# Gates to rows and back by small transfers and block transposes, in a hybrid attention block

## The chip, the core and the metric

One Trainium2 chip; the kernel runs on one of its cores. The metric is device time in microseconds of one execution. A core has five engines that are named here as the profile names them: PE (TensorE, matrix products; PEld is its weight loads), DVE (VectorE), ACT (ScalarE), POOL (GpSimd) and SP (SyncE). Each runs its own queue of instructions in order, and they wait for each other by semaphores. POOL and SP also issue transfers (DMA) on queues of their own.

## What is computed

The reference is one block of a network: a root mean square norm of x (256 tokens of 4096), a projection into three kinds of token mixing (an mLSTM, a sparse attention, a gated delta rule), and a projection back that is added to x.

```python
h = rms_norm(x, norm_g[l])
proj = jnp.einsum('bsd,dn->bsn', h, w_in[l])
(aq, ak, av, ai, af, ao, az, bcq, bk, bv, bki, bwi, bz,
 cqkv, cb, ca, cz) = jnp.split(proj, split_points, axis=-1)
h_a = mlstm_chunked(..., soft_cap(ai + m_ib[l]), soft_cap(af + m_fb[l]))
...
beta = jax.nn.sigmoid(cb)
g = -jnp.exp(d_a_log[l]) * jax.nn.softplus(ca + d_dt_bias[l])
o_c = gated_delta_chunked(q_c, k_c, v_c, g, beta)
...
x = x + jnp.einsum('bsm,md->bsd', y, w_out[l])
```

The gates ai, af, cb and ca are 8 columns each, one for each head. They need running sums and maxima over the 256 tokens, and end as factors of one token and one head.

## The kernel before

**Chunks and gaps.** The work is a list of 46 blocks of matrix product, each over 512 columns (496 for the block with the gates), cut into 536 chunks of two 128-row slices of the weights. A chunk is 12 matmuls on PE: two slices, two halves of the tokens, and three products of high and low parts (L1039, L1041, L1042). SP loads raw weights (w_raw, four buffers). ACT rounds them to w_hi (`split_hi`, L1313), DVE makes the rest w_lo (`split_lo`, L1650), both three chunks ahead of PE and with four buffers, so ACT can make w_hi of chunk c+3 only when PE has done with chunk c-1. Products go to two accumulators; after a block's last chunk ACT reads its accumulator with the norm's factor (`evac`).

**What sets the order.** `plan` writes everything else by hand into gaps: `woven[c]` lists the pieces that stand after chunk c on every engine. In slot c ACT first does w_hi of c+3, then its parts of the pieces of `woven[c]`; DVE likewise with w_lo; PE does chunk c and then its parts. `weave(at, pieces, every)` puts pieces in gaps from `at` on. `end(kind)` is the last chunk of a block. The block with the gates is block 6 and ends with chunk 111; block 7, the first of two with a Silu, ends with chunk 127.

**The pieces around the change.** `evac` of block 6 writes the gates to `small` (128 tokens on partitions, 2 halves, 112 columns). `csq` and `cn` take squares of q and k and sum them on PE; ACT's part of cn i is a Ln of PE's sum (L1428). `ce` takes Exp on ACT (L1432) and multiplies on DVE (L1807, L1809). The gates go through seven steps:
- gt: PE turns `small` by eight transposes into rows (L1010), one head on each of 8 partitions and 256 tokens along it; ACT reads them from PE's banks with Tanh, Exp, Identity and Ln (L1375 to L1387) into `rows`.
- g1 (DVE, with a reciprocal, L1710 to L1713), g2 (ACT, Exp and Ln, L1391, L1392), g3 (DVE, running sums and maxima, L1719 to L1736), g4 (ACT, two Exp, L1396, L1399).
- gb: PE turns `rows` back by nine transposes; DVE copies them to `gcol` (L1740), and with ACT makes `gder`.

POOL writes rows 1 to 3 to `rows_dram` (L812) when g3 is done and spreads them to all partitions for `ca` (L818, L819). ca, cg, vd, kn and all that follow, down to a place in block 15, are laid out from where gb stands. Ahead of that POOL moves the values of the heads to memory and back for a block transpose (v_dram, L800, L805), in two halves `hg`. ACT loads a table of functions before Tanh or Exp, before Ln and before Silu when another is in place.

```python
def gt(_, use):                       # PE
    wait_stored(pe, "gates", 512)
    for i in range(4):
        u = use + i // 2
        ...
        for m in range(M):
            ins = turn(bank(u)[0:8, (i % 2) * SEQ + m * P:(i % 2) * SEQ + m * P + P],
                       small[:, m, 8 * i:8 * i + 8])
```

## Time and profile before

| what | us |
|---|---|
| median of three timed runs | 1539.94 (1539.55 to 1540.01) |
| the profiled execution | 1541.16 |
| its span | 1539.4 |
| PE busy | 1534.1 |
| DVE busy | 994.4 |
| ACT busy | 753.0 |
| POOL busy | 353.2 |

The profile is of one execution. A timeline gives the instructions of an engine in order of their start; matmuls are pipelined, so their lengths overlap and the cost of one is read from the starts. In brackets stands how long the engine was idle before an instruction and what released it. The granted clock of PE was full in every slice.

### The profile page before, as it was taken

The numbers are of one execution on the slowest core, as the hardware profiler recorded it, in microseconds if no ns is written. First come the engines' busy times: TensorE is split into PE (matmuls) and PEld (weight loads), VectorE is DVE, ScalarE is ACT, GpSimd is POOL, SyncE is SP. The second block draws the span as 40 slices with busy tenths as digits, with TensorE's granted clock in tenths as the row PEclk, the third lists the DMA queues.
The fourth block names the chain that finished last, engine by engine and source line by source line (L and its number), as shares of the span: only waits on it lengthen the run. The fifth ranks groups of instructions, "written<-read, shape, count | busy, mean of one in ns | idle before, by whom it ended". The sixth has DMA issues, their size and how long they took to land.

```text
span 1539.4 us, 18848 instructions
## 1 busy us (share of the span) xinstructions
PE 1534.1 (100%) x7000; PEld 1271.0 (83%) x7000; DVE 994.4 (65%) x1536; ACT 753.0 (49%) x1006; POOL 353.2 (23%) x601
## 2 busy tenths in 40 slices
PE   9999999999999999999999999999999999999999
PEld 7888888888888888888878888888888888888887
DVE  6647555657769855576579667675456676664554
ACT  6745444587543444554545545535346444443332
POOL 8041112230230040127410355345300120200000
PEclk9999999999999999999999999999999999999999
DMA  9886778886786685558756787799885776666674
GB/s 287 282 244 198 222 212 229 204 244 189 222 251 211 193 223 163 165 179 277 243 171 201 222 236 217 223 267 260 256 247 178 245 223 190 210 199 194 195 249 153
DMA packets 206283, 337.51 MB, mean 219 GB/s; under 512 B 52937, under 2 KB 60664, under 8 KB 205936
## 3 DMA queue, kind: packets, MB, share of 16 engines
q1 hardware_dynamic: 185056, 288.66, 62.1%
q0 software_dynamic: 21088, 47.63, 11.8%
q8 instruction: 55, 0.90, 0.2%
q14 instruction: 36, 0.29, 0.1%
q10 hardware_dynamic: 48, 0.02, 0.0%
HBM read 312.55 MB, written 23.49 MB: 218 GB/s over the span
## 4 chain that ended last, share of the span: by engine, by line
PE 98%; DVE 1%; ACT 0%; issue 0%; DMA 0%; DVEq 0%
PE acc L1039 31%; PE acc L1042 31%; PE acc L1041 31%; PE mix L1102 1%; PE mix L1175 1%; PE mix L1095 0%; PE mix L1164 0%; PE mix L1010 0%; PE acc L1243 0%; DVE w_lo L1650 0%; PE mix L1161 0%; PE mix L1151 0%; ACT w_hi L1313 0%; PE mix L1149 0%; PE mix L1185 0%
## 5 line engine op out<-in xcount | busy, mean ns | idle before, releaser
L1650 DVE TENSOR_TENSOR w_lo<-w_raw,w_hi 128x1024 fp32r<-128x1024 f32 (+2 forms) x535 | 645.8, 1218 | 424.9 <-ACT w_hi L1313 421.6
L1313 ACT ACTIVATE w_hi<-w_raw 128x1024 fp32r<-128x1024 f32 (+2 forms) x535 | 556.3, 1050 | 532.9 <-PE acc L1042 446.4
L1039 PE MATMUL acc<-w_hi,op_hi 128*128 128x512 f32 (+1 forms) x2036 | 801.0, 393 | 0.3 <-DVE w_lo L1650 0.3
L1042 PE MATMUL acc<-w_hi,op_lo 128*128 128x512 f32 (+1 forms) x2036 | 793.9, 390 | 0.0
L1041 PE MATMUL acc<-w_lo,op_hi 128*128 128x512 f32 (+1 forms) x2036 | 792.9, 389 | 0.0
L1039 PEld LDWEIGHTS acc<-w_hi,op_hi 128*128 128x128 f32 x2036 | 382.6, 188 | 80.3 <-issue 1.6
L1042 PEld LDWEIGHTS acc<-w_hi,op_lo 128*128 128x128 f32 x2036 | 382.3, 188 | 80.2
L1041 PEld LDWEIGHTS acc<-w_lo,op_hi 128*128 128x128 f32 x2036 | 382.7, 188 | 77.3
L783 POOL DMA_DIRECT2D conv_dram<-y x48 | 30.6, 690 | 169.7 <-ACT y L1365 168.9
L783 POOL DMA_DIRECT2D y_dram<-y x32 | 20.5, 712 | 181.9 <-DVE y L2089 115.1
L937 POOL DMA_DIRECT2D bp_dram<-b_ps x48 | 31.4, 710 | 70.2 <-ACT b_ps L1534 66.7
L783 POOL DMA_DIRECT2D bq_dram<-qs x32 | 20.5, 713 | 75.6 <-DVE qs L1957 75.6
L1534 ACT ACTIVATE b_ps<-b_s,st 128x128 f32<-128x128 f32 (+1 forms) x32 | 14.3, 446 | 46.4 <-DVE st L2030 46.3
L948 POOL DMA_DIRECT2D b_pT<-bp_dram x48 | 26.4, 567 | 39.4 <-DMA bp_dram<-b_ps 39.4
L1039 PE MATMUL acc<-w_hi,cq_hi 128*128 128x512 f32 x84 | 33.6, 399 | 0.0
L1041 PE MATMUL acc<-w_lo,cq_hi 128*128 128x512 f32 x84 | 33.4, 398 | 0.0
L1042 PE MATMUL acc<-w_hi,cq_lo 128*128 128x512 f32 x84 | 33.1, 394 | 0.0
L789 POOL DMA_DIRECT2D y<-conv_dram x48 | 25.4, 539 | 22.2 <-DMA conv_dram<-y 22.2
L1000 POOL DMA_DIRECT2D out_dram<-acc x2 | 1.5, 726 | 125.9 <-DVE acc L1677 125.9
L1785 DVE SCALAR_TENSOR_TENSOR cT<-y,par,cT 128x255 f32<-128x255 f32 (+2 forms) x72 | 29.4, 479 | 0.0
L858 POOL DMA_DIRECT2D lane_out_dram<-lane_u x4 | 4.2, 1064 | 106.4 <-DVE lane_u L1846 106.4
L994 POOL DMA_DIRECT2D y<-in_x_dram x6 | 4.2, 710 | 92.7 <-DVE op_lo L2110 92.7
(348 smaller groups left out, 991.9 us busy)
## 6 DMA issues: line engine op xcount, KB each, us to landing
w_raw<-in_w_in_dram SPq DMA_DIRECT2D x367, 512.0 KB, 4.6
w_raw<-in_w_out_dram SPq DMA_DIRECT2D x128, 512.0 KB, 4.5
w_raw<-in_w_in_dram SPq DMA_DIRECT2D x16, 384.0 KB, 3.3
w_raw<-in_a_wuq_dram SPq DMA_DIRECT2D x12, 512.0 KB, 5.4
conv_dram<-y POOLq DMA_DIRECT2D x48, 64.0 KB, 3.9
y<-conv_dram POOLq DMA_DIRECT2D x48, 64.0 KB, 4.9
w_raw<-in_a_wuqi_dram SPq DMA_DIRECT2D x6, 512.0 KB, 4.3
bp_dram<-b_ps POOLq DMA_DIRECT2D x48, 64.0 KB, 4.3
```

Of the source, the lines that this page charges most:

```text
L783: pool.dma_start(*kept_block(dst, src, m, i)).then_inc(signal, 16)
L789: pool.dma_start(*moved_block(dst, src, q, j)).then_inc(signal, 16)
L937: pool.dma_start(bp_dram[n % 2][:, :, :, i, :].rearrange("a k j b -> a (k j) b"), b_ps[32 * i:32 * i + 32, n % 2].rearrange("p (f b) -> p ...
L948: pool.dma_start(b_pT[32 * j:32 * j + 32, n % 2], bp_dram[n % 2][:, :, j].rearrange("a k i b -> a k (i b)")).then_inc(bp_moved[n % 2], 16)
L1039: nc.tensor.matmul(o, hi[:, kt, tok], hv[:, i, n0:n1], start=(kt == (kts if late else blk["kts"])[0]), stop=False)
L1041: nc.tensor.matmul(o, hi[:, kt, tok], lv[:, i, n0:n1], start=False, stop=False)
L1042: last_mm = nc.tensor.matmul(o, lo[:, kt, tok], hv[:, i, n0:n1], start=False, stop=(kt == blk["kts"][-1]))
L1102: ins = nc.tensor.matmul(bank(use)[:, a * n:a * n + n], lhs(a), rhs(a), start=True, stop=True)
L1175: ins = nc.tensor.matmul(bank(use)[:, o * P:o * P + P], b_pT[:, (3 * g + v) % 2, i, :], val, start=(v == 0 or i % 2 == 0), stop=(v == 0 or ...
L1313: func(split_ap(w_hi, c), w_raw[:, c % RAW_BUFS, 0:n], ACT.Copy).then_inc(hi_ready, 1)
L1650: vec.tensor_tensor(split_ap(w_lo, c), w_raw[:, c % RAW_BUFS, 0:n], split_ap(w_hi, c).bitcast(F32), ALU.subtract).then_inc(lo_ready, 1)
L1785: ins = vec.scalar_tensor_tensor(cT[:, c, d:SEQ], conv_columns(i, j)[:, 0:SEQ - d], par[:, row:row + 1], cT[:, c, d:SEQ], ALU.mult, ALU.add)
```

## The change

The gates are no longer turned by PE. A new piece gs on DVE transposes the 32 gate columns of `small` in blocks of 32x32, in place; POOL writes them to memory with four transfers (`g_dram`) in such an order that a row of 256 tokens is contiguous, and reads them into `rows` with four. gt is then ACT's alone and reads `rows`. On the way back POOL writes rows 0, 4 and 5 too, and brings them into `small` and a new tile `gates5` in blocks with eight transfers; DVE transposes both in place and copies them to `gcol`. The steps stand in other gaps:

| piece | gap before | gap now |
|---|---|---|
| gs | none | 112 |
| gt | 120 | 118 |
| g1 | 122 | 119 |
| g2 | 124 | 120 |
| g3 | 126 | 122 |
| g4 | 128 | 124 |
| gb | 130 | 129 |
| evac of block 7 | 127 | 129 |
| ca 0, and all pieces after it down to bkt and yd 13 | 132 to 258 | one gap earlier |

csq, cn and ce stay where they were. Four semaphores of the first chunk become two with the same order of waits. The diff, cut:

```diff
-USES = {"par": 2, "gt": 2, "gb": 1, "kx": 1, ...
+USES = {"par": 2, "kx": 1, ...
     for b, x in enumerate(blocks):
-        woven[last[b] if b else FIRST_EVAC].append(("evac", b))
+        late = 2 if x["kind"] == "silu" and x["arg"] == W_A + W_B else 0
+        woven[last[b] + late if b else FIRST_EVAC].append(("evac", b))
-    g_end = weave(max(at, end("gates", 512) + 2), [(name, 0) for name in ("gt", "g1", "g2", "g3", "g4", "gb")], 2)
+    gates = end("gates", 512)
+    for name, slot in (("gs", 1), ("gt", 7), ("g1", 8), ("g2", 9), ("g3", 11), ("g4", 13), ("gb", 18)):
+        weave(gates + slot, [(name, 0)])
+    g_end = gates + 20
...
# POOL, behind the first four v_dram transfers of hg == 1
+                    pool.wait_ge(g_dve, 1)
+                    for i in range(4):
+                        pool.dma_start(g_dram[:, :, i, :], small[32 * i:32 * i + 32, :, 0:32]).then_inc(g_kept, 16)
...
+            pool.wait_ge(g_kept, 16 * 4)
+            for r, g in ((0, G_AI), (1, G_AF), (3, G_CB), (2, G_CA)):
+                pool.dma_start(rows[:, r, :], g_dram[g:g + 8].rearrange("c m i t -> c (m i t)")).then_inc(g_moved, 16)
             wait_read(pool, "cn", 7)
             clear_corners(1)
-            pool.wait_ge(g_dve, 3)
-            pool.dma_start(rows_dram[:].rearrange("r h t -> h r t"), rows[:, 1:4, :]).then_inc(rows_kept, 16)
-            pool.wait_ge(rows_kept, 16)
+            pool.wait_ge(g_dve, 4)
+            pool.wait_ge(g_rows, 2)
+            pool.dma_start(rows_dram[0:3].rearrange("r h t -> h r t"), rows[:, 1:4, :]).then_inc(rows_kept, 16)
+            pool.dma_start(rows_dram[3], rows[:, 0, :]).then_inc(rows_kept, 16)
+            pool.dma_start(rows_dram[4], rows[:, 4, :]).then_inc(rows_kept, 16)
+            pool.dma_start(rows_dram[5][:, 0:P], rows[:, 5, 0:P]).then_inc(rows_kept, 16)
+            pool.wait_ge(rows_kept, 16 * 4)
+            for i in range(4):
+                pool.dma_start(small[32 * i:32 * i + 32, :, 0:32], rows_dram[1:5]...[:, :, i, :]).then_inc(g_moved, 16)
+                pool.dma_start(gates5[32 * i:32 * i + 8, :], rows_dram[5][:, 32 * i:32 * i + 32]).then_inc(g_moved, 16)
...
# PE: gt and gb are gone
...
# ACT
             def gt(_, use):
-                wait_filled(act, use)
+                act.wait_ge(g_moved, 16 * 4)
                 act.wait_ge(head_ready, 1)
-                func(rows[:, 0, :], b[0:8, 0:SEQ], ACT.Tanh, ...)
...
+                func(rows[:, 0, :], rows[:, 0, :], ACT.Tanh, bias=hcol[:, 4:5], scale=1 / GATE_CAP).then_inc(g_act, 1)
+                step(func(rows[:, 1, :], rows[:, 1, :], ACT.Tanh, bias=hcol[:, 5:6], scale=1 / GATE_CAP))
+                step(func(rows[:, 1, :], rows[:, 1, :], ACT.Exp, scale=-GATE_CAP))
...
# DVE
+            def gs(_, use):
+                wait_stored(dve, "gates", 512)
+                step(vec.memset(gates5[:], 0.0))
+                vec.transpose(small[:, :, 0:32], small[:, :, 0:32]).then_inc(g_dve, 1)
             def gb(_, use):
-                wait_filled(dve, use)
-                done_bank(vec.tensor_copy(gcol[:].rearrange("p a b -> p (a b)"), bank(use)[:, 0:72]), use)
+                dve.wait_ge(g_moved, 16 * (4 + 8))
+                step(vec.transpose(small[:, :, 0:32], small[:, :, 0:32]))
+                step(vec.transpose(gates5[:], gates5[:]))
+                vec.tensor_copy(gcol[:, 4, :], gates5[:, 0:8])
+                for i, q in ((0, 0), (5, 2)):
+                    ins = vec.tensor_copy(...)
+                step(ins)
```

The order of ACT's queue, from cn 6 (c_bt from a bank, Ln) on. Before: the w_hi rows are those of chunks 122, 123 and, at the end, 124, the rows pieces between are gt.

```order
246 L1428 ACTIVATE c_bt<-mix,eps 128x512 [waits filled2]
247 L1313 ACTIVATE w_hi<-w_raw 128x1024 [waits split_used,raw_ready2]
248 L1428 ACTIVATE c_bt<-mix,eps 128x512 [waits filled3]
249 L1313 ACTIVATE w_hi<-w_raw 128x1024 [waits split_used,raw_ready3]
250 L1375 ACT_TABLE_LOAD [waits head_ready]
251 L1375 ACTIVATE rows<-mix,hcol 8x256 [waits filled0]
252 L1376 ACTIVATE rows<-mix,hcol 8x256
253 L1379 ACTIVATE rows<-rows 8x256 [waits emptied0]
254 L1383 ACTIVATE rows<-mix 8x256 [waits filled1]
255 L1384 ACTIVATE rows<-mix,hcol 8x256
256 L1387 ACT_TABLE_LOAD
257 L1387 ACTIVATE rows<-rows 8x256 [waits emptied1]
```

Now, from the same cn 6: the w_hi rows are those of chunks 122, 123 and 124.

```order
246 L1422 ACTIVATE c_bt<-mix,eps 128x512 [waits filled2]
247 L1376 ACT_TABLE_LOAD [waits head_ready]
248 L1376 ACTIVATE rows<-rows,hcol 8x256 [waits g_moved]
249 L1377 ACTIVATE rows<-rows,hcol 8x256
250 L1378 ACTIVATE rows<-rows 8x256 [waits act_step]
251 L1379 ACTIVATE rows<-rows 8x256 [waits act_step]
252 L1380 ACTIVATE rows<-rows,hcol 8x256
253 L1381 ACT_TABLE_LOAD
254 L1381 ACTIVATE rows<-rows 8x256 [waits act_step]
255 L1316 ACTIVATE w_hi<-w_raw 128x1024 [waits split_used,raw_ready2]
256 L1422 ACTIVATE c_bt<-mix,eps 128x512 [waits filled3]
257 L1316 ACTIVATE w_hi<-w_raw 128x1024 [waits split_used,raw_ready3]
```

gt stands ahead of w_hi of 122 instead of behind w_hi of 123, and waits for transfers (g_moved) instead of PE's banks. g2 is next:

```order
258 L1385 ACT_TABLE_LOAD
259 L1385 ACTIVATE rows<-rows 8x256 [waits g_dve]
260 L1386 ACT_TABLE_LOAD
261 L1386 ACTIVATE rows<-rows 8x256 [waits act_step]
262 L1316 ACTIVATE w_hi<-w_raw 128x1024 [waits split_used,raw_ready0]
263 L1426 ACT_TABLE_LOAD
264 L1426 ACTIVATE c_kb<-c_kb 128x512 [waits emptied0]
```

It stands ahead of w_hi of 124 and of ce 0, where before w_hi of 125, 126 and 127 and three ce stood ahead of it.

DVE's queue from the last csq_lo on. Before, the four w_lo are those of chunks 121 to 124:

```order
174 L1799 TENSOR_TENSOR csq_lo<-kv,csq_hi 128x512 [waits c_sq]
175 L1650 TENSOR_TENSOR w_lo<-w_raw,w_hi 128x1024 [waits hi_ready] x4
176 L1807 SCALAR_TENSOR_TENSOR cT<-cT,c_kb 128x512 [waits c_r]
177 L1650 TENSOR_TENSOR w_lo<-w_raw,w_hi 128x1024 [waits hi_ready]
178 L1710 TENSOR_SCALAR rows<-rows 8x256 [waits g_act]
179 L1711 RECIPROCAL rows<-rows 8x256 [waits dve_step]
180 L1713 SCALAR_TENSOR_TENSOR rows<-rows 8x256 [waits emptied1,dve_step]
181 L1807 SCALAR_TENSOR_TENSOR cT<-cT,c_gam 128x512 [waits c_r]
182 L1650 TENSOR_TENSOR w_lo<-w_raw,w_hi 128x1024 [waits hi_ready]
183 L1807 SCALAR_TENSOR_TENSOR cT<-cT,c_vk 128x512 [waits c_r]
184 L1650 TENSOR_TENSOR w_lo<-w_raw,w_hi 128x1024 [waits hi_ready]
185 L1807 SCALAR_TENSOR_TENSOR cT<-cT,c_vk 128x512 [waits c_r]
```

Now the w_lo rows are those of chunks 121 and 122, then 123 and 124, then 125, and g3 begins with the row of L1712:

```order
176 L1802 TENSOR_TENSOR csq_lo<-kv,csq_hi 128x512 [waits c_sq]
177 L1644 TENSOR_TENSOR w_lo<-w_raw,w_hi 128x1024 [waits hi_ready] x2
178 L1704 TENSOR_SCALAR rows<-rows 8x256 [waits g_act]
179 L1705 RECIPROCAL rows<-rows 8x256 [waits dve_step]
180 L1706 SCALAR_TENSOR_TENSOR rows<-rows 8x256 [waits dve_step]
181 L1644 TENSOR_TENSOR w_lo<-w_raw,w_hi 128x1024 [waits hi_ready] x2
182 L1810 SCALAR_TENSOR_TENSOR cT<-cT,c_kb 128x512 [waits c_r]
183 L1644 TENSOR_TENSOR w_lo<-w_raw,w_hi 128x1024 [waits hi_ready]
184 L1712 SCALAR_TENSOR_TENSOR rows<-rows 8x256 [waits g_act]
185 L1713 TENSOR_SCALAR rows<-rows,hcol 8x256 [waits dve_step]
186 L1716 SCALAR_TENSOR_TENSOR rows<-ones,rows 8x128 [waits dve_step] x2
187 L1723 SCALAR_TENSOR_TENSOR rows<-ones,rows 8x256 [waits g_dve]
```

Between g1 and g3 stood four w_lo and four ce before; now there are three w_lo and one ce.

## Rows read from the trace of the kernel before

**Rows 1.** The page, busy us, share of the span and instructions of each engine.

```profile
PE 1534.1 (100%) x7000; PEld 1271.0 (83%) x7000; DVE 994.4 (65%) x1536; ACT 753.0 (49%) x1006; POOL 353.2 (23%) x601
```

**Rows 2.** PE's timeline at gt (start, length, engine, line, tiles, form); then tile small.

```profile
336.43 0.39 PE L1083 MATMUL mix<-csq_hi,ones 128*128 128x512 f32 x1
...
339.61 0.39 PE L1083 MATMUL mix<-csq_hi,ones 128*128 128x512 f32 x1
...
340.06 0.39 PE L1039 MATMUL acc<-w_hi,op_hi 128*128 128x512 f32 x1
...
342.78 1.03 PE L1010 MATMUL mix<-ident,small 128*8 128x128 f32 x8
...
345.26 0.39 PE L1041 MATMUL acc<-w_lo,op_hi 128*128 128x512 f32 x1
...
L1010 PE MATMUL mix<-ident,small x8: 271/273/273, 342.8 to 343.5; 128*8 128x128 f32 x8
```

**Rows 3.** PE's timeline around gb.

```profile
371.26 0.39 PE L1042 MATMUL acc<-w_hi,op_lo 128*128 128x512 f32 x1
...
373.96 0.39 PE L1041 MATMUL acc<-w_lo,op_hi 128*128 128x512 f32 x1
```

**Rows 4.** PE's timeline where chunk 130 begins; in brackets the idle time and its releaser.

```profile
367.93 0.39 PE L1042 MATMUL acc<-w_hi,op_lo 128*128 128x512 f32 x1
368.64 0.50 PE L1039 MATMUL acc<-w_hi,op_hi 128*128 128x512 f32 x1 [0.32 <-DVE w_lo L1650]
...
370.13 0.39 PE L1039 MATMUL acc<-w_hi,op_hi 128*128 128x512 f32 x1
```

**Rows 5.** ACT's timeline from cn 6 to the end of g2.

```profile
337.08 0.69 ACT L1428 ACTIVATE c_bt<-mix,eps 128x512 f32<-128x512 f32 x1 [0.72 <-PE mix L1084]
...
343.42 0.46 ACT L1375 ACTIVATE rows<-mix,hcol 8x256 f32<-8x256 f32 x1 [0.22 <-PE mix L1010]
...
346.94 1.04 ACT L1313 ACTIVATE w_hi<-w_raw 128x1024 fp32r<-128x1024 f32 x1
...
349.29 0.63 ACT L1432 ACTIVATE c_kb<-c_kb 128x512 f32<-128x512 f32 x1
349.83 1.05 ACT L1313 ACTIVATE w_hi<-w_raw 128x1024 fp32r<-128x1024 f32 x1
...
354.58 0.42 ACT L1391 ACTIVATE rows<-rows 8x256 f32<-8x256 f32 x1 [0.77 <-DVE rows L1713]
...
356.74 1.28 ACT L1432 ACT_TABLE_LOAD   x1
```

**Rows 6.** DVE's timeline from g1 on, with its nearest copy and transposes.

```profile
352.05 0.27 DVE L1710 TENSOR_SCALAR rows<-rows 8x256 f32<-8x256 f32 x1
...
362.53 0.41 DVE L1719 SCALAR_TENSOR_TENSOR rows<-rows 8x256 f32<-8x256 f32 x1
...
366.78 0.67 DVE L1809 TENSOR_TENSOR cT<-cT,c_bt 128x512 f32<-128x512 f32 x1
367.38 1.20 DVE L1650 TENSOR_TENSOR w_lo<-w_raw,w_hi 128x1024 fp32r<-128x1024 f32 x1
368.52 0.67 DVE L1809 TENSOR_TENSOR cT<-cT,c_bt 128x512 f32<-128x512 f32 x1
...
373.13 0.21 DVE L1740 COPY gcol<-mix 128x72 f32<-128x72 f32 x1
...
385.43 1.30 DVE L1795 STREAM_TRANSPOSE cT<-cT 128x512 f32<-128x512 f32 x2
```

**Rows 7.** POOL's timeline; then DMA issues of 332.4:333.2 and 366:385, us to landing.

```profile
330.67 2.32 POOL L805 DMA_DIRECT2D cT<-v_dram  x4 [5.88 <-DMA v_dram<-cT]
...
367.48 0.58 POOL L812 DMA_DIRECT2D rows_dram<-rows  x1 [25.38 <-DVE cT L1809]
...
cT<-v_dram POOLq DMA_DIRECT2D x2, 128.0 KB, 6.5
...
rows_dram<-rows POOLq DMA_DIRECT2D x1, 24.0 KB, 2.0
```

## What I predicted, and why

> **What bounds the kernel now.** I read the page first: the span is 1539.4 us and PE is busy for 1534.1 us of it [rows 1]. The page warns that a busy PE need not be at its peak, so I read PE's timeline around the places that the change touches. Chunk 120 begins at 340.06 and what follows it at 342.78 [rows 2]: 12 matmuls in 2.72 us, 0.227 each, without a gap. PE therefore sets the end, and only three things can move the time: fewer PE instructions, a PE stall that goes, a PE stall that comes.
>
> Then come the stalls. There is one in this stretch: chunk 130 should have begun at 367.93 + 0.23 = 368.16, and begins at 368.64, when DVE delivers the low half of its weights [rows 4]. Seven matmuls later 370.13 stands where 368.16 + 6 x 0.227 = 369.52 would have: 0.61 us lost, of which 0.48 is the waiting and 0.13 the restart.
>
> Why DVE was late there is the key to this case. ACT makes w_hi of chunk c+3 and DVE its w_lo before either does the pieces of gap c, so each piece there eats into a lead over PE. A rows piece is thin (8 partitions), yet g3 alone takes DVE from 362.53 to 366.78, 4.25 us [rows 6], against 2.72 us of PE per chunk.
>
> **What is removed.** gt on PE: the eight turns of small begin at 342.78 and the eighth matmul of the next chunk at 345.26, where without them it would begin at 342.78 + 7 x 0.227 = 344.37. That is 0.89 us [rows 2]. gb on PE: the last matmul before it begins at 371.26, the eighth after it at 373.96, without the turns 371.26 + 8 x 0.227 = 373.08. That is 0.88 us [rows 3]. Together 1.77 us, certain, since PE is on the path. If the stall at 368.16 goes too, 0.61 us more: at most 2.38 us.
>
> Here a rule of the Trainium skill (TensorE: Matmul & The Clock Gate, Part 4: PE-mode transpose) would promise more: it gives about 275 ns to a transpose in a kernel's context. Each of the eight turns is indeed 0.273 long in its own row, but they overlap, and by the starts they cost 0.11 each [rows 2], so the trace agrees with the duration and not with the cost; 17 at 275 ns would be 4.7 us instead of 1.77 us.
>
> **What is added, and hidden.** On DVE: gs (a memset and a block transpose of 128x64) in gap 112; gb becomes two transposes and three copies. None of these shapes is in the trace. From below they are bounded by the 0.21 us that a 128x72 copy takes, from above by the 1.30 us of two 128x512 transposes plus three such copies, 1.9 us [rows 6]. I take 0.4 for gs and 1.3 for gb. DVE waits in gap 112 for ACT anyway, and by the chain below chunk 133 is still over 2 us ahead at gb: both are hidden, at either end. On POOL: 19 issues more (4 + 4, then 3, then 8), each near the 0.58 us of the rows_dram transfer [rows 7], 11 us in all. The first four lie in the 5.88 us that POOL waited for v_dram, the last eleven in a stretch where it waited 25.38 us [rows 7]. The return trip: DVE's g3 and ACT's g4 are done at about 359.9, four issues 2.3, landing 2.0, eight issues 4.6, landing 2.0 gives 370.8, and DVE reaches gb at about 371.9. Hidden; landings may be some 3 us longer before PE notices. The spreads of c_kb then start at about 368.8 against 369.8 before, one gap ahead of their reader, as before. From ca on everything is one gap earlier, with the same distances; no stall is in the trace there, and I add none. Silu's read of block 7 moves from gap 127 to 129: its bank is wanted again only at chunk 144, so nothing waits for it, and its two table loads leave the crowded gaps. Cost nothing.
>
> **What is moved: the chain of gates.** This is the term that decides. gt goes from gap 120 to 118, g1 from 122 to 119, g2 from 124 to 120, g3 from 126 to 122. The ten gaps between gt and the end of DVE's work behind g3 become eight, and ACT stands at gt later relative to PE: the piece before it, cn 6, waits for PE at the end of chunk 118 (it starts at 337.08 [rows 5]). I follow the chain by start times, with durations from the rows before:
> - Tanh starts when rows have landed or the table is loaded, 337.08 + 0.57 + 1.28 = 338.93. When do the rows land? POOL's last cT transfers of the head values are issued from 330.67 on, the four rows transfers behind them at about 333.0 to 335.3, and these wait in the same queue. The lone rows_dram transfer landed in 2.0 us, the last cT transfers in 6.5 [rows 7]. From 334.7 that is 336.7 to 341.2. The DMA engines are full there, so I take 5.0: 339.7.
> - From Tanh to the next w_hi it took 343.42 to 346.94, 3.52 [rows 5]; one more wait for ACT's own write, 0.13: w_hi of 122 at 343.4.
> - w_hi is 1.04 long, with its signal 1.07, so w_lo of 122 starts at 344.45; it holds DVE for 1.14 (367.38 to 368.52 [rows 6]), so g1 starts at 345.6.
> - g1 until ACT's Exp: 352.05 to 354.58, 2.53; Exp, table load, Ln: 354.58 to 356.74, 2.16 [rows 5], less 0.1 of overlap: w_hi of 124 at 350.15. It waits behind g2 on ACT's queue; PE wants chunk 124 at 350.9.
> - w_hi 0.95, table load 1.28, ce 0 at 352.4; 0.54 later w_hi of 125 (349.29 to 349.83), 1.07 later its w_lo at 354.0, 1.14 later g3 at 355.15.
> - g3 4.25, ce 1 0.60 (366.78 to 367.38), w_lo of 126 with its signal 1.25 [rows 6]: ready at 361.25.
>
> PE without waits: chunk 119 begins at 336.43 + 0.45, and with cn 7's 0.45 chunk 126 would begin at 336.88 + 7 x 2.72 + 0.45 = 356.37. So PE is late by 4.9 us there. By the same chain it first waits a little for chunks 122 to 124 (0.2, 0.7, 0.4) and 3.2 us for 126; with restarts 5.0 us in all. After that DVE has no g piece until gap 129 and gains 0.9 us per chunk. As a test, the same step-by-step reckoning with the order of before gives w_lo of 130 at 368.5 and one wait for chunk 130, which is what the rows show [rows 4].
>
> **The sum.** -0.89 - 0.88 - 0.61 + 5.0 = +2.6 us. The profiled execution took 1541.16 us around its span of 1539.4; the median of the three timed runs is 1539.94, 1.2 lower. On the profiled one it makes 1543.8, on the median 1542.5, which I predict. The bounds of the landing give +1.9 (anything up to 338.93) and +4.1 (341.2).
>
> A second rule that bears on the chain is in the Trainium skill (ScalarE: Activation LUTs, What ACT_TABLE_LOAD costs): a switch costs about 2.66 us, of which 1.38 is a drain. Here a load takes 1.28 and the next ACTIVATE follows at once [rows 5], so the trace speaks against the drain; with it three loads in the chain would add 4 us.
>
> **The rivals.**
> - Late rows, slower beyond what can be told: ACT stands at Tanh with w_hi of 122 queued behind it, and each us after 338.93 goes to PE one to one. The point is a landing after 340.2, where the sum passes 3.08 us. For it: the 6.5 us of the transfers just ahead. Against: 8 descriptors of 1 KB are little. At 341.2 it gives +4.1, 1544.0. Chance 0.35.
> - No pile-up: ACT or DVE are further ahead than I reckon (gt's wait for cn 6 shorter, or g1 and g2 overlapping with the splits more). Then the turns and the old stall go and nothing comes: -2.4, 1537.5. Against it: g1, g2, g3 and three splits in a row are 21.5 us of serial work for 19.5 of PE's. Chance 0.07. Half-way (between -1.5 and +1.8) 0.16.
> - Turns priced one by one: each of gt's eight held PE for its own 0.273, 2.2 us, and gb's nine by the same ratio 2.2, and with the pile-up the sum is -4.4 - 0.6 + 5.0 = 0, 1539.9. Against it stand the starts in [rows 2, 3]. Chance 0.02. (Part 4 of the Trainium skill's page, TensorE: Matmul & The Clock Gate, prices them so.)
> - It does not do what it says: DVE waits at gb for the eight small transfers. This needs landings over 3 us longer, then about +1 on top. Within the range; no chance of its own.
>
> **How the numbers follow.** The forecast (rows in time, pile-up, +1.8 to +3.08) has 0.37, late rows 0.35, the same sign by a chain that is longer than I reckon 0.03, half-way 0.16, no pile-up 0.07, the page's price 0.02. A measurement tells 0.2% from no change, 3.08 us. Faster by that needs more than all three terms can give. I leave 0.02 for it, taken from the no pile-up case. Slower by it is the late rows and the longer chain: 0.38. The rest, 0.60, lies within. The range leaves out 0.1 at each end: from -1.2 (1538.7) to +5.5 (1545.4), which takes in both landings and half a us of error in the chain.
>
> **What would show it.** After: no turns of small or rows on PE; PE idle before the first matmul of chunks 122 to 124 and 126, released by DVE's w_lo, the longest about 3 us until about 361, after g3; no wait at chunk 130; Tanh released by the DMA of rows, not by the table load. Wrong, if PE has no idle between 340 and 365, if Tanh starts before 339, or if DVE reaches g3 more than 2 us earlier than 355.

## The result, and the profile after

The changed kernel took 1545.11 us (median of 8 runs, 1543.84 to 1545.89) where the kernel before took 1540.93 beside it (8 runs): a ratio of 1.0026, with an interval of 1.0017 to 1.0035. It is 4.2 us slower. That lies within the range and has the sign of the forecast of +2.6, but it is 1.6 us more, as much as one term that the forecast did not have. (The 1542.5 of the forecast stands on three runs of the kernel before with a median of 1539.94; beside the changed kernel it took 1.0 us more.) The profiled execution has a span of 1543.9 us. Of all the runs below one, of experiment 6, was in a slow state (2039.65 us at a granted clock of 0.706), and it stays out of the ratios.

PE's busy time grew by 0.3 us although 17 of its instructions are gone. The page of the changed kernel, answering to [rows 1]:

```profile
PE 1534.4 (99%) x6983; PEld 1271.5 (82%) x6983; DVE 995.1 (64%) x1542; ACT 754.2 (49%) x1006; POOL 364.2 (24%) x620
```

The whole trace of the changed kernel is 2.02 us late from the first chunk on: 1.1 us of it come from PE's first transpose, which waited 1.30 us for norm_in instead of 0.20, and the rest from the first matmuls behind it, which stand wider apart in this execution (start, length, engine, line, tiles, form, in brackets the idle time and its releaser):

```profile
4.51 0.28 PE L1032 MATMUL mix<-ident,norm_in 32*128 32x32 f32 x1 [1.30 <-DMA norm_in<-in_norm_g_dram]
```

So 2.02 has to be taken off wherever a time of after is set beside one of before. PE's timeline of the changed kernel through the stretch of the gates, and its list of waits in the whole execution (us in total, times, longest):

```profile
347.29 0.39 PE L1064 MATMUL acc<-w_hi,op_lo 128*128 128x512 f32 x1
347.83 0.50 PE L1061 MATMUL acc<-w_hi,op_hi 128*128 128x512 f32 x1
...
351.80 0.50 PE L1061 MATMUL acc<-w_hi,op_hi 128*128 128x512 f32 x1 [0.93 <-DVE w_lo L1644]
...
355.04 0.50 PE L1061 MATMUL acc<-w_hi,op_hi 128*128 128x512 f32 x1 [0.19 <-DVE w_lo L1644]
...
360.56 0.39 PE L1064 MATMUL acc<-w_hi,op_lo 128*128 128x512 f32 x1
363.90 0.50 PE L1061 MATMUL acc<-w_hi,op_hi 128*128 128x512 f32 x1 [2.95 <-DVE w_lo L1644]
364.24 0.59 PE L1063 MATMUL acc<-w_lo,op_hi 128*128 128x512 f32 x1
364.62 0.63 PE L1064 MATMUL acc<-w_hi,op_lo 128*128 128x512 f32 x1
...
367.61 0.43 PE L1061 MATMUL acc<-w_hi,op_hi 128*128 128x512 f32 x1
367.88 0.39 PE L1063 MATMUL acc<-w_lo,op_hi 128*128 128x512 f32 x1
```

```profile
PE acc L1061 <- DVE w_lo L1644: 4.1, 3, 3.0
```

These are the chunks 122 (0.31 late, without a bracket), 123, 124 and 126. Chunk 130 has no wait any more. What comes behind the long wait was in no term of mine: from 364.24 on the matmuls follow each other at up to 0.43 us instead of 0.227. A view by stretches of time shows why (length, PE busy, granted clock, DMA share, GB/s):

```profile
361.00:363.90 2.90, 0.00 (x0) 1.00 0.00 0
363.90:365.00 1.10, 1.10 (x3) 0.67 0.33 36
365.00:366.00 1.00, 1.00 (x4) 0.50 0.76 166
...
368.30:370.00 1.70, 1.70 (x9) 1.00 0.89 264
```

The granted clock went from 1.00 to 0.50, that is from 2.4 to 1.2 GHz, behind an idle stretch of 2.95 us, and came back at 367.6. From 364.24 to 367.88 nine matmuls took 3.64 us where nine at 0.227 take 2.04: 1.6 us.

The chain of the gates on ACT and DVE, answering to [rows 5, 6]:

```profile
339.81 1.28 ACT L1376 ACT_TABLE_LOAD   x1
341.63 0.51 ACT L1376 ACTIVATE rows<-rows,hcol 8x256 f32<-8x256 f32 x1 [0.54 <-DMA rows<-g_dram]
...
345.47 1.04 ACT L1316 ACTIVATE w_hi<-w_raw 128x1024 fp32r<-128x1024 f32 x1
...
350.64 0.42 ACT L1385 ACTIVATE rows<-rows 8x256 f32<-8x256 f32 x1 [1.31 <-DVE rows L1706]
...
352.69 1.04 ACT L1316 ACTIVATE w_hi<-w_raw 128x1024 fp32r<-128x1024 f32 x1
```

```profile
347.69 0.69 DVE L1704 TENSOR_SCALAR rows<-rows 8x256 f32<-8x256 f32 x1
...
356.66 1.23 DVE L1644 TENSOR_TENSOR w_lo<-w_raw,w_hi 128x1024 fp32r<-128x1024 f32 x1 [0.26 <-ACT w_hi L1316]
357.80 0.41 DVE L1712 SCALAR_TENSOR_TENSOR rows<-rows 8x256 f32<-8x256 f32 x1
...
362.04 0.67 DVE L1810 SCALAR_TENSOR_TENSOR cT<-cT,c_gam 128x512 f32<-128x512 f32 x1
362.64 1.21 DVE L1644 TENSOR_TENSOR w_lo<-w_raw,w_hi 128x1024 fp32r<-128x1024 f32 x1
...
376.29 0.23 DVE L1738 STREAM_TRANSPOSE small<-small 128x64 f32<-128x64 f32 x1
```

g1 begins at 347.69, and its first instruction is 0.69 us long where [rows 6] have 0.27. DVE does g3 from 357.80 to 362.04, and only then a piece of 0.6 us and w_lo of chunk 126. At gb (376.29) it waits for nothing, though only just: the last of the small transfers, issued at 372.01, took 4.0 us to land. Pool's timeline, answering to [rows 7], and under it how long the transfers took to land (the us at the end of a line):

```profile
334.61 2.10 POOL L820 DMA_DIRECT2D rows<-g_dram  x4
...
347.14 1.10 POOL L783 MEMSET y<- 64x512 f32 x2 [10.43 <-ACT c_bt L1422]
...
363.23 0.62 POOL L826 DMA_DIRECT2D rows_dram<-rows  x1 [14.98 <-ACT rows L1393]
...
368.25 0.57 POOL L832 DMA_DIRECT2D small<-rows_dram  x1 [2.86 <-DMA rows_dram<-rows]
```

```profile
rows<-g_dram POOLq DMA_DIRECT2D x4, 8.0 KB, 5.1
...
small<-rows_dram POOLq DMA_DIRECT2D x4, 8.0 KB, 3.5
gates<-rows_dram POOLq DMA_DIRECT2D x4, 1.0 KB, 3.8
```

### The profile page after: what moved, and what is told of

Its sections match the earlier page's. It is cut to its first block, busy times and chain, and to the rows that moved or that the text cites. A ratio compares the mean times of both kernels' runs of the same rounds, so it can differ in the third digit from the quotient of the medians.

```text
span 1543.9 us, 18835 instructions
## 1 busy us (share of the span) xinstructions
PE 1534.4 (99%) x6983; PEld 1271.5 (82%) x6983; DVE 995.1 (64%) x1542; ACT 754.2 (49%) x1006; POOL 364.2 (24%) x620
## 4 chain that ended last, share of the span: by engine, by line
PE 95%; DMA 1%; DVE 1%; ACT 1%; POOL 1%; issue 0%; ACTq 0%; DVEq 0%
PE acc L1061 30%; PE acc L1064 30%; PE acc L1063 30%; PE mix L1105 1%; DMA v_dram<-cT 1%; PE mix L1178 1%; DVE w_lo L1644 0%; PE mix L1167 0%; PE mix L1098 0%; ACT w_hi L1316 0%; PE acc L1246 0%; DMA rows<-g_dram 0%; DVE cT L1788 0%; POOL cT L815 0%; POOL v_dram L806 0%
```

## The experiments

**Theory.** The order of the gate steps costs the time, by a long wait of PE for w_lo behind g3 and by the lower clock that follows the wait; the transfers themselves cost nothing. **Rivals.** The transfers cost time through a late landing; or the slow matmuls are not a matter of the wait; or the merged semaphores of the first chunk or the later read of block 7 do something. To compare two traces I took the start of the first matmul of each slice of weights in both: their difference, from slice to slice, is where time comes or goes, and is called the offset here.

**1. The merged semaphores alone.** The kernel before, with only

```diff
-        first_x_hi = sem("first_x_hi")
-        first_x_lo = sem("first_x_lo")
-        first_w_hi = sem("first_w_hi")
-        first_w_lo = sem("first_w_lo")
+        first_hi = sem("first_hi")
+        first_lo = sem("first_lo")
```

and the waits that go with them.

> The kernel before with only the first chunk's four semaphores merged into two, as in the changed kernel. In the changed kernel's profile PE's first product of chunk 0 came 1.1 us later and the whole trace ran 2.0 us behind from there. Theory (chance): the late landing of norm_in is chance, the semaphores cost nothing: ratio 1.000, within 0.1%, and the profile shows no stall between 16 and 340 us. Rival (the merging costs): about 2 us, ratio 1.0013, and the matmuls of chunk 0 wait longer than before for the second count of the merged semaphore.

1540.76 us, ratio 1.0001 (0.9992 to 1.001). No effect that these runs can tell.

**2. The order alone.** The kernel before with PE's turns and none of the transfers, but with the steps in the gaps of the changed kernel:

```diff
+        late = 2 if x["kind"] == "silu" and x["arg"] == W_A + W_B else 0
+        woven[last[b] + late if b else FIRST_EVAC].append(("evac", b))
...
+    for name, slot in (("gt", 7), ("g1", 8), ("g2", 9), ("g3", 11), ("g4", 13), ("gb", 18)):
+        weave(gates + slot, [(name, 0)])
+    g_end = gates + 20
```

> The kernel before, PE's transposes kept and no transfer added, but the gates' steps in the changed kernel's gaps (gt 118, g1 119, g2 120, g3 122, g4 124, gb 129, Silu's read of block 7 at 129). Theory (the order of the steps costs, not the transfers): Tanh starts at 338.9, PE waits about 3 us for chunk 126, the wait at chunk 130 is gone; 1.0 to 1.7 us more if PE's clock falls after that idle time as it did in the changed kernel; in all +2.5 to +4.5 us on the kernel before (1.0016 to 1.003). Rival (the small transfers and their landing cost): the order alone is hidden, ratio 0.9995 to 1.0005.

1545.58 us (five runs), ratio 1.0032 (1.002 to 1.0045): all of the loss, without one of the new transfers. PE's turns are still in it: by the offset it loses 5.5 us up to chunk 153, where the changed kernel, without them, loses 4.7. PE's timeline of this kernel, and its view by stretches:

```profile
360.84 0.79 PE L1043 MATMUL acc<-w_hi,op_hi 128*128 128x512 f32 x1 [2.90 <-DVE w_lo L1654]
361.43 0.63 PE L1045 MATMUL acc<-w_lo,op_hi 128*128 128x512 f32 x1
...
363.99 0.39 PE L1045 MATMUL acc<-w_lo,op_hi 128*128 128x512 f32 x1
```

```profile
361.00:364.00 3.00, 3.00 (x8) 0.51 0.65 181
```

The same wait, and the same fall of the clock; here the first matmul after the wait is already slow (0.79 against 0.50). So neither belongs to the transfers.

**3. Is the clock a cost of its own?** The changed kernel, with PE kept at work where it would be idle: 25 turns of the identity ahead of chunk 126, into a bank that nobody reads.

```diff
-    for name, slot in (("gs", 1), ("gt", 7), ("g1", 8), ("g2", 9), ("g3", 11), ("g4", 13), ("gb", 18)):
+    for name, slot in (("gs", 1), ("gt", 7), ("g1", 8), ("g2", 9), ("g3", 11), ("g4", 13), ("wm", 14), ("gb", 18)):
...
+            def wm(_, use):
+                wait_emptied(pe, use)
+                for i in range(24):
+                    ins = turn(bank(use)[:, 0:P], ident[:])
+                end_fill(ins, use)
+                turn(bank(use)[:, 0:P], ident[:]).then_inc(emptied[use % 4], 1)
```

> The changed kernel, with 25 turns of the identity (128x128 into a bank that nobody reads) on PE just ahead of chunk 126, whose weights come 2.95 us late in the trace of the changed kernel. At some 0.11 us a turn they take 2.8 us: PE works through the idle stretch instead of waiting, and chunk 126 starts when it did. Nothing else changes. Theory (the clock): it was the idle stretch behind which the granted clock fell to 0.50 for 3.7 us, and this cost 1.7 us; with PE busy the clock stays at 1.00, the matmuls behind it keep their pitch of 0.227 us, and the time is 1.7 us below the changed kernel's, about 1543.3. Rival (the slow matmuls come from something else in that stretch, as the load of the memories or the engines there): matmuls at 0.43 us remain and the time stays at 1545.1.

1542.99 us, ratio 1.0012 (1.0003 to 1.0021), 2.1 us below the changed kernel by the medians of two sets of runs, 1.7 expected (the two intervals overlap, from 1.0017 to 1.0021, so I rest this on the trace). PE's and DVE's timelines and one stretch of this kernel:

```profile
359.25 2.89 PE L1032 MATMUL mix<-ident 128*128 128x128 f32 x25
362.36 0.50 PE L1061 MATMUL acc<-w_hi,op_hi 128*128 128x512 f32 x1 [0.22 <-DVE w_lo L1651]
...
374.39 0.24 DVE L1745 STREAM_TRANSPOSE small<-small 128x64 f32<-128x64 f32 x1 [1.16 <-DMA gates<-rows_dram]
```

```profile
363.00:364.00 1.00, 1.00 (x6) 1.00 0.63 70
```

Chunk 126 starts no sooner (its offset, less that of the start, is 4.61 in both kernels), yet the clock stays at 1.00 and the matmuls at 0.227, and two chunks later the offset is 4.74 where the changed kernel has 6.34. Useless work on an idle PE saved the 1.6 us. This shows that the idle PE brought the clock down, and what it cost. It shows one thing more: with DVE some 1.5 us sooner at gb, DVE stands there 1.16 us for the small transfers, which it did not in the changed kernel.

**4. Less waiting.** The changed kernel with g3 two gaps later, g4 and gb one, the C pieces where they stood before:

```diff
-    for name, slot in (("gs", 1), ("gt", 7), ("g1", 8), ("g2", 9), ("g3", 11), ("g4", 13), ("gb", 18)):
+    for name, slot in (("gs", 1), ("gt", 7), ("g1", 8), ("g2", 9), ("g3", 13), ("g4", 14), ("gb", 19)):
...
-    g_end = gates + 20
+    g_end = gates + 21
```

> The changed kernel with only g3 two gaps later (124), g4 125 and gb 130, all after it as in the kernel before; gt, g1 and g2 stay at 118, 119 and 120. Theory (PE waits because DVE has no lead left at g3, and regains some 0.9 us per chunk): the waits for chunks 122 to 124 stay, the long one moves to chunk 128 and is about 1.2 us instead of 3.0; PE's granted clock stays at 2.4 GHz after it, so the 1.7 us of slow matmuls go too: 3.5 us under the changed kernel, about 1.000 to 1.001 of the kernel before. Rival (the long wait comes from a transfer or from g3's own input, not from the lead): it stays at about 3 us and moves with g3.

1540.82 us, ratio 1.0001 (0.9992 to 1.001); the long wait is now at chunk 128 and 1.07 us, the granted clock 1.00 through the stretch.

**5. One gap later** lies between the two: g3 in slot 12, nothing else moved.

```diff
-    for name, slot in (("gs", 1), ("gt", 7), ("g1", 8), ("g2", 9), ("g3", 11), ("g4", 13), ("gb", 18)):
+    for name, slot in (("gs", 1), ("gt", 7), ("g1", 8), ("g2", 9), ("g3", 12), ("g4", 13), ("gb", 18)):
```

> The changed kernel with DVE's g3 one gap later (at 123) and nothing else moved. The chain then reaches w_lo of chunk 127, not 126, and PE has one more chunk's work ahead of it: the long wait moves to chunk 127 and is 2.2 us where it was 2.95. The waits before it (0.9 and 0.2) stay. Less waiting is worth 1.0 us. It also asks from what wait on the clock falls, since waits of 0.93 and 1.07 us left it at 1.00 and those of 2.90 and 2.95 us did not. If 2.2 us is long enough: a stretch at 0.50 behind it again, time 1544.1. If it is not: 1542.4.

1542.57 us, ratio 1.0011 (1.0002 to 1.002). PE's timeline and a stretch:

```profile
364.73 0.50 PE L1061 MATMUL acc<-w_hi,op_hi 128*128 128x512 f32 x1 [1.97 <-DVE w_lo L1644]
365.07 0.40 PE L1063 MATMUL acc<-w_lo,op_hi 128*128 128x512 f32 x1
```

```profile
364.70:368.00 3.30, 3.27 (x14) 1.00 0.71 178
```

In the profiled execution one gap took 1.0 us off the wait and with it the whole fall of the clock: the branch of 1542.4 in the expectation. It was not so in every execution. Each run has a mean granted clock; it is 1.000 in eight of the eleven, as in the profiled one, and 0.999 in three, as in the changed kernel. The median of the eight is 1542.49 us, that of the three 1543.38.

**6. The landing alone.** The changed kernel with Pool's queue in another order, every step in its gap:

```diff
             for hg in range(2):
+                if hg == 1:
+                    pool.wait_ge(g_dve, 1)
+                    for i in range(4):
+                        pool.dma_start(g_dram[:, :, i, :], small[32 * i:32 * i + 32, :, 0:32]).then_inc(g_kept, 16)
...
                 if hg == 1:
-                    pool.wait_ge(g_dve, 1)
-                    for i in range(4):
-                        pool.dma_start(g_dram[:, :, i, :], small[32 * i:32 * i + 32, :, 0:32]).then_inc(g_kept, 16)
+                    pool.wait_ge(g_kept, 16 * 4)
+                    for r, g in ((0, G_AI), (1, G_AF), (3, G_CB), (2, G_CA)):
+                        pool.dma_start(rows[:, r, :], g_dram[g:g + 8].rearrange("c m i t -> c (m i t)")
...
-            pool.wait_ge(g_kept, 16 * 4)
-            for r, g in ((0, G_AI), (1, G_AF), (3, G_CB), (2, G_CA)):
-                pool.dma_start(rows[:, r, :], g_dram[g:g + 8].rearrange("c m i t -> c (m i t)")).then_inc(g_moved, 16)
```

> The changed kernel with only Pool's queue re-ordered: the gate columns leave ahead of the second half of v and the rows come ahead of v's return, so they land some 4 us sooner. Every step stays in its gap. It prices the landing, which the rival of the late rows makes the cause. Theory (the landing is a small term and the packed chain the large one): Tanh is then released by its table load behind cn 6, 0.5 us sooner than in the changed kernel, and the long wait of PE at chunk 126 is 2.95 - 0.5 = 2.4 us, which still stands: -0.5 us, 1544.6, if the clock falls behind it as behind 2.95; 1542.9, if it stays up as behind 1.97. Rival (the landing decides): the long wait goes, 1539 or below.

1543.14 us (1542.87 without the run of 2039.65), ratio 1.0013 (1.0004 to 1.0022), at the lower of the expected 1544.6 and 1542.9, and far from the 1539 of the rival. ACT's and PE's timelines and two stretches of this kernel, whose trace is 0.36 us early against before from the start:

```profile
338.72 0.51 ACT L1378 ACTIVATE rows<-rows,hcol 8x256 f32<-8x256 f32 x1
```

```profile
361.00 0.80 PE L1063 MATMUL acc<-w_hi,op_hi 128*128 128x512 f32 x1 [2.94 <-DVE w_lo L1646]
```

```profile
360.00:361.00 1.00, 0.00 (x0) 0.56 0.00 0
...
365.00:366.00 1.00, 1.00 (x4) 0.50 0.94 332
```

Tanh now waits for its table only, 0.5 us sooner. I had the wrong place for the gain: it is the 0.31 us wait at chunk 122 and its restart that went, and the long wait stayed (2.94, not 2.4). Up to the start of chunk 126 the kernel gained 0.52 us on the changed one (offset less that of the start: 4.09 against 4.61), so a late landing does pass to PE one to one; it was just small. In this profiled execution the clock was down longer, until 366.9, which cost 2.8 us there against 1.6 with the changed kernel. That execution is not typical: its mean granted clock is 0.998, where four of the other runs have 0.999 and five have 1.000, no fall that shows. Those five have a median of 1542.03 us, the five with a fall 1543.74. So both branches of the expectation came, in different executions of one kernel.

**7. The steps further apart.** The changed kernel with g1 three gaps behind gt, g2 three behind g1, gb at 131:

```diff
+    for name, slot in (("gs", 1), ("gt", 7), ("g1", 10), ("g2", 13), ("g3", 14), ("g4", 16), ("gb", 20)):
...
+    g_end = gates + 21
```

> The changed kernel with the gates' steps further apart: gt 118, g1 122 instead of 119 (gap 121), g2 124, g3 125, g4 127, gb 131, and all that follows where it stood in the kernel before. To be exact: g1 in gap 121, g2 124, g3 125, g4 127, gb 131. The transfers and block transposes are the changed kernel's. Theory (the crowding of g1, g2 and g3 costs): no wait of PE over 0.4 us between 340 and 420, no fall of the clock there, and the two turns and the old wait at chunk 130 are saved: -1 to -2.4 us on the kernel before (0.9985 to 0.9994), some 6 us under the changed kernel. Rival (the transfers cost wherever the steps stand): as slow as the changed kernel, 1.002 or more; or DVE waits at gb for the small transfers and PE behind it for chunks 135 and 136.

1539.83 us, ratio 0.9994 (0.9986 to 1.0003): less than the 2.4 us of the turns and the old wait. The waits at 122 to 126 went, all but 0.18 us at 122 (and 0.20 at 129), but a new one came. DVE's, ACT's and PE's timelines:

```profile
378.22 0.24 DVE L1738 STREAM_TRANSPOSE small<-small 128x64 f32<-128x64 f32 x1 [4.45 <-DMA gates<-rows_dram]
```

```profile
379.33 0.22 ACT L1397 ACTIVATE gder<-gcol 128x16 f32<-128x16 f32 x1 [5.52 <-DVE gder L1745]
```

```profile
400.27 0.50 PE L1061 MATMUL acc<-w_hi,op_hi 128*128 128x512 f32 x1 [1.08 <-DVE w_lo L1644]
```

Here g4 comes later and gb can't follow (behind it stand pieces that may not be later than before), so the return trip shows: Pool issues its first transfer at 364.40, DVE gets the last at 378.22, 13.8 us later. DVE stands 4.45 us at gb, the lead is lost, and PE waits some 20 us later, at chunk 140. Another wait, of 0.67 us at 1120.16, is far from the change; of the other kernels only that of experiment 8 has its like, and its cause is not shown.

**8. Both cures together.** The early rows of experiment 6 allow gt one gap sooner, and with it all others:

```diff
+    for name, slot in (("gs", 1), ("gt", 6), ("g1", 8), ("g2", 12), ("g3", 13), ("g4", 14), ("gb", 20)):
...
+    g_end = gates + 21
```

> The changed kernel with two things moved. On Pool's queue the four transfers of the gate columns go out ahead of the second half of v, and the four that bring the rows ahead of those that bring v back; the rows then land some 4 us sooner, and the steps may start one gap sooner. The steps stand at gaps 117 (gt), 119 (g1), 123 (g2), 124 (g3), 125 (g4) and 131 (gb), so that ACT's table loads and DVE's 2.4 and 4.2 us have free gaps between them. Theory (the changed kernel lost by the order of the steps alone, and the transfers do save PE's turns): no wait of PE from chunk 118 to 140, no fall of the clock, the turns' 1.77 us and the old wait's 0.61 us saved: 1538.5. Rival (the transfers have a price of their own, in DVE and ACT waiting for the return trip at gb, as in the kernel with the steps spread out, where the lead was lost and PE waited 1.1 us at chunk 140): 1539.8 or above, with a wait of PE at or behind chunk 136.

1538.46 us, ratio 0.9981 (0.9973 to 0.999), where 1538.5 was expected: faster than both kernels. Its page, and PE's one wait in the stretch:

```profile
PE 1532.0 (100%) x6983; PEld 1270.1 (83%) x6983; DVE 995.2 (65%) x1542; ACT 753.6 (49%) x1006; POOL 362.4 (24%) x620
```

```profile
363.33 0.47 PE L1063 MATMUL acc<-w_hi,op_hi 128*128 128x512 f32 x1 [0.34 <-DVE w_lo L1646]
```

One wait of 0.34 us was left that I had not expected, behind g3, and there is one of 0.50 us at 1118.80, far from the change. At gb DVE waits 0.18 us for the small transfers.

**9. The same order with PE's turns.** The kernel before, no transfers, with the gaps of experiment 8 (slots 6, 8, 12, 13, 14, 20, and the read of block 7 at gap 129):

> The kernel before, PE's turns kept and no transfers, with the gate steps in the gaps of the fastest kernel so far (gt 117, g1 119, g2 123, g3 124, g4 125, gb 131, the read of block 7 at 129). Beside that kernel it leaves the transfers as the only difference. Theory: the order of the steps removes the old wait and its restart (0.6 us) and the turns still cost PE their 1.77 us: 1540.3, that is 1.8 us above the kernel with early rows and spread steps (1538.5). Rival (the spread order alone brought the gain and the turns lie in idle time): 1538.5 here too.

1540.15 us, ratio 0.9998 (0.9989 to 1.0006), as expected within 0.2. The old wait at chunk 130 is gone, but PE is held up for 0.26 us and a restart at chunk 140 instead:

```profile
400.09 0.39 PE L1046 MATMUL acc<-w_hi,op_lo 128*128 128x512 f32 x1
400.58 0.50 PE L1043 MATMUL acc<-w_hi,op_hi 128*128 128x512 f32 x1
```

By the medians the transfers are worth 1.7 us once the order is right, by the ratios of the two sets of runs 2.6. By the offsets up to chunk 153: -1.61 with transfers, -0.03 without.

**10. The read of block 7 alone**, in the kernel before at gap 129, and **11.** in the changed kernel put back to 127.

```diff
-        woven[last[b] if b else FIRST_EVAC].append(("evac", b))
+        late = 2 if x["kind"] == "silu" and x["arg"] == W_A + W_B else 0
+        woven[last[b] + late if b else FIRST_EVAC].append(("evac", b))
```

> The kernel before with one thing of the change: ACT reads block 7 two gaps later, at gap 129. PE's turns, the gate steps and their gaps are those of before. It prices this part by itself. Theory: PE's wait of 0.32 us at chunk 130 and the restart behind it go, 0.6 us, since ACT gets to w_hi of chunk 130 ahead of the 2.7 us of table load and reads: 1540.3, ratio 0.9996. Rival: ACT is only late two gaps further on, and the wait comes back at chunk 132: 1541.0.

1540.44 us, ratio 0.9997 (0.9988 to 1.0005). Nothing changed in the trace, and my expectation of 0.6 us was wrong: the wait at chunk 130 stands as before, in a trace that is 1.37 us later.

```profile
370.01 0.50 PE L1040 MATMUL acc<-w_hi,op_hi 128*128 128x512 f32 x1 [0.32 <-DVE w_lo L1651]
```

> The changed kernel with the read of block 7 put back to gap 127, where it stands in the kernel before. In the kernel before, this move by itself changed nothing: the wait of 0.32 us at chunk 130 stayed. Theory (the read's two table loads fall where ACT has time, behind the long wait of chunk 126): the same as the changed kernel, 1545.1, the long wait 2.95 us again. Rival (the later read hides 2.7 us of ACT's work while it is behind): one more wait at chunk 130, of 1 us or more, and 1546 or above.

1544.27 us, ratio 1.002 (1.0011 to 1.0029), the waits 0.61, 0.95, 0.23 and 2.91, and the clock down behind the last. No wait at chunk 130, so it isn't the read's place that removes it there. What is common to all kernels without the wait of 0.32 us (the changed one and experiments 2 to 9, 11 and 12) is that DVE does g3 one to four gaps sooner than at 126.

**12. The first instruction of g1.** In all traces it is 0.69 or 0.70 us long where Pool's two memsets of its corners lie beside it (the changed kernel's from 347.14 to 348.24), and 0.27 in the kernels where they had ended 2 us or more ahead (10 us in the kernel before, 2.1 in experiment 7). The changed kernel with them later:

```diff
             wait_read(pool, "cn", 7)
+            pool.wait_ge(g_dve, 2)
             clear_corners(1)
```

> The changed kernel, with Pool clearing its corners (two memsets, 1.10 us) only when g1 is done on DVE; there it ran at the same time as the first instruction of g1. That instruction took 0.69 us in each of the kernels where the memsets lay beside it and 0.27 in the two (the kernel before and the loosely spread one) where they had ended 3 us or more ahead of it. Theory (the two hold each other up): it takes 0.27 us here, the chain of the gates is 0.42 us shorter, PE waits 0.42 us less at chunk 123, and since PE then comes to chunk 126 sooner by as much as the chain, the long wait stays 2.9 us with the clock down behind it: 0.4 us less, 1544.7, where only the trace can tell it. Rival (its length comes from ACT's writing of rows or from its place behind w_lo): 0.69 us again and every wait as in the changed kernel.

1543.97 us, ratio 1.0018 (1.0009 to 1.0027). DVE's and PE's timelines of this kernel:

```profile
345.57 0.27 DVE L1705 TENSOR_SCALAR rows<-rows 8x256 f32<-8x256 f32 x1
```

```profile
349.25 0.50 PE L1062 MATMUL acc<-w_hi,op_hi 128*128 128x512 f32 x1 [0.52 <-DVE w_lo L1645]
```

The instruction is back at 0.27 and the wait at chunk 123 is 0.41 us shorter (0.52 against 0.93): shown. Up to chunk 126 only 0.25 us of it are left, since the rows landed 0.18 us later in this execution. The long wait is 2.91 us and the clock falls in it, as expected; by their mean granted clock it fell in six of the eleven runs (median 1544.76 us) and not in the other five (1543.18).

## Why the prediction was right, and what it missed

The sum is best read by the offset between the traces (the time of before is given, the common delay of 2.02 taken out):

| term | forecast, us | measured, us |
|---|---|---|
| gt's turns gone (at 343) | -0.89 | -0.90 |
| waits and restarts, chunks 122 to 126 (345 to 357) | +5.0 | +5.6 |
| matmuls at 1.2 GHz (357 to 363) | none | +1.6 |
| old wait and gb's turns gone (to 375) | -0.61 - 0.88 | -1.49 |
| up to chunk 153 (to 440) | none | -0.14 |
| sum | +2.6 | +4.7 |

**The turns.** Right to 0.01 us for gt; with the old wait the rest is right to a hundredth. The price by starts, 0.11 us a turn [rows 2], held, not the turn's own length, and the rival that prices them one by one falls: 0.90 and not 2.2 us.

**The landing.** Issued at 334.61, which is 332.6 in before's time (333.0 forecast), landed in 5.1 us (5.0 forecast, a choice between 2.0 and 6.5, so in part luck), Tanh at 339.61 (339.7). The rival of the late rows had the mechanism right, one to one, as experiment 6 shows; its condition, a landing after 340.2, was not met, and its branch is not what made the time, though the time itself, +4.2, is the one that it gave (+4.1).

**The chain.** The forecast was made of start times, and these can be checked one by one, each less 2.02: w_hi of 122 at 343.45 (343.4), Exp of g2 at 348.62 (348.09), w_hi of 124 at 350.67 (350.15), w_hi of 125 at 353.56 (352.9), g3 at 355.78 (355.15), w_lo of 126 ready at 361.83 (361.25). Up to g1 it is right to a tenth; 0.42 us came in g1, whose first instruction ran into Pool's memsets (experiment 12), and stayed to the end. I had copied g1's length from [rows 6] without asking what Pool does at the new place. (The 21.5 us held against the rival of no pile-up are the whole way from Tanh to w_lo of 126, with gt in it, and not g1, g2, g3 and three splits alone.) The cost of the waits is made of how late the four chunks start (0.31, 1.09, 0.35 and 3.11 us by the starts of the matmuls; the brackets say up to 0.16 less, since the last matmul's end is modelled) and of four restarts at 0.11 to 0.17: 5.45 of the 5.6 us; the rest lies at chunk 125, which began 0.03 us late and had a restart too. Forecast were 0.2, 0.7, 0.4, 3.2 and 0.13 each.

**The missed term.** The sum carried every matmul behind the wait at 0.227 us. I took PE's pace as a constant of the kernel and did not ask what 3.2 us of idle PE do to it. The long wait cost 3.11 us, a restart of 0.11, and 1.6 us more. With that term the sum would have been +4.2, as the medians have it; that this agrees to a tenth is luck, since 0.6 more of waiting and, by the medians, 0.5 less in the rest of the execution cancel in it. Experiments 2, 3 and 5 show the term from three sides.

**The cause of the old wait.** That it goes was right; the prediction counted on the freed gaps in general and named the two table loads of block 7's read among them. Experiments 10 and 11 show that the read has no part in it.

**The return trip.** Forecast as hidden, and hidden it was, by luck. The landings of the eight transfers took 3.4 to 4.0 us instead of 2.0, and the last came at 373.95 in before's time where 370.8 was forecast, 3.1 us later. DVE, forecast at gb at 371.9, came at 374.27, 0.3 us behind that landing, and it was that late because of the terms that the forecast had too small or not at all. Where PE got there sooner, DVE did wait: 1.16 us in experiment 3, with every step in the same gap, 2.45 in experiment 5 and 1.66 in experiment 4. PE noticed none of these three (no wait of PE from chunk 129 to 140), so the bound that I gave, some 3 us until PE notices, was not reached. In experiment 7, with 4.45 us at gb, it was. The rival of DVE waiting at gb is real, and I gave it no chance of its own; what it costs PE depends on how long DVE stands there. The spreads of c_kb, forecast one us sooner than before (368.8), began 0.7 us later (370.50), and no wait of PE came of it.

**The rest of the execution.** The spans differ by 4.5 and the medians by 4.2. Behind chunk 153 the changed kernel gains 2.2 us, and it had lost 2.02 at the very start, by chance: the kernels with the same code there begin between 0.37 us ahead of before and 2.02 behind it (experiment 1: 0.53 behind). Of the 2.2, 1.1 lie at 977 us, where the profiled execution of before has an idle time of 0.86 us ("issue") at PE's line 1161 and that of experiment 10 has 0.58, while in experiment 1, with the same order, most of it is missing; I take this for chance. Another 0.4 to 0.5 comes in small steps between 500 and 970 us, in every kernel with transfers and in none of the four without. So it goes with the transfers, but what makes it stays open. The remaining 0.6 lies in small steps behind 977 us. Of these, 0.25 at 1225 us stand in the comparison of before with every other kernel, also that of experiment 1, so they belong to the profiled execution of before; for the rest I have no cause.

## What to carry to other kernels

A piece that is taken off the bounding engine is worth its spacing, not its length, and can lose all of it to the order in which what remains is put: here 1.8 us of turns against 5.6 us of waits that came because a serial chain over three engines was packed into eight gaps instead of ten. Where a forecast has a wait of PE of the size of those that brought the clock down here, add what the lower clock behind it costs, and look first for a neighbouring gap that shortens the wait: the first microsecond taken off saved two and a half here, by the medians. When steps are spread out or a wait is removed, follow the transfers to their reader again: a return trip may have been hidden only because its reader was late.

## What the runs showed of the hardware

In the profiled executions the granted clock fell from 1.00 to 0.50 with waits of PE of 2.90, 2.91 (twice), 2.94 and 2.95 us, and did not with waits of 0.93, 1.07, 1.08 and 1.97 us. By the stretches it fell before work resumed in experiments 2, 6, 11 and 12, and just after in the changed kernel, and it stayed down while PE was at work again. The cost came in two sizes, 1.3 to 1.6 us (the changed kernel, experiments 2 and 11) and 2.8 us (experiments 6 and 12).

The same kernel does not do the same in each execution. The mean granted clock of a run is 1.000 where the profile shows no fall, 0.999 where it shows one of the first size and 0.998 where it shows one of the second. By it the clock fell in all eight runs of the changed kernel and all five of experiment 2, in ten of eleven of experiment 11, six of eleven of experiment 12, five of ten of experiment 6, three of eleven of experiment 5, and none of eleven of experiment 3, where PE was kept at work. The changed kernel has one run at 0.998 among its eight, experiment 2 two of five, so the size of the fall varies between executions as well; what decides it is not shown. Inside one kernel the runs with a fall took 1.6 us more (experiment 12) and 1.7 us more (experiment 6) by the medians, which agrees with the price of experiment 3. One run of the kernel before has a mean of 0.949 at an ordinary 1541.35 us, so that number alone does not give a time.

While the clock was down in the changed kernel, matmuls of 512 columns followed each other at 0.427 us (364.62 to 367.18 in six steps). The Trainium skill (TensorE: Matmul & The Clock Gate, "Wait — 56ns, not 53.3ns?") gives 426.7 ns for this at 1.2 GHz, and the rows agree; for 2.4 GHz it gives 215.7 ns, where the rows of this kernel have 227.

A small DVE instruction was held up beside a memset of Pool: it begins at 347.69 and ends at 348.38, 0.69 us where it takes 0.27 alone, and the memsets end at 348.24. The Trainium skill (SBUF — State Buffer, "SBUF: two separate sides") says that a Pool instruction and a DVE instruction in a mode that uses two ports lock a shared pair of ports against each other for a whole instruction. This trace and experiment 12 agree with it, 0.42 us each time; that the DVE instruction was in such a mode no trace shows.

The small transfers on Pool's queue took 3.5 us (8 KB), 3.8 us (1 KB) and, among large ones, 5.1 us (8 KB) to land, the lone one of before 2.0 [rows 7]: four to eight of them, issued 0.5 us apart, took 1.5 to 3 us more each. The first of the four writes to rows_dram (24 KB) took 2.1 us in the changed kernel, those issued right behind it (8 and 4 KB) 3.1 to 3.4.
